# First block of a two-layer kernel: the recurrence, the index with its top-k and the attention run in pieces between the parts of one input product of 19 reordered groups

## Time and profile before

| What | Value |
|---|---|
| Median of 3 runs (lowest to highest) | 2316.65 us (2316.13 to 2317.55) |
| The profiled execution's own time | 2318.26 us |
| Its span | 2316.5 us |
| Mean granted clock of TensorE, share of full speed | 0.941 |
| PE busy / DVE busy / ACT busy / POOL busy | 92% / 62% / 38% / 1% |
| Input product, first to last matmul | 127.86 to 545.27 us |
| Output product g_o, first matmul | 718.04 us |

### The profile page before, as it was taken

The page is one execution under the profiler, slowest core; times in us unless marked ns, Lnnn a source line. Parts: engine busy times, 40 slices in busy tenths (PEclk is TensorE's granted clock), DMA queues, the critical chain, the costliest instruction groups (busy, mean ns, idle before and its releaser), DMA issues.

```text
span 2316.5 us, 23790 instructions
## 1 busy us (share of the span) xinstructions
PE 2122.0 (92%) x9261; PEld 1678.0 (72%) x9261; DVE 1438.8 (62%) x2254; ACT 884.3 (38%) x1070; POOL 21.5 (1%) x13
## 2 busy tenths in 40 slices
PE   6799999996697989999996779898999999999999
PEld 1278888885465867788783458777888888878887
DVE  4478655667837877787778676646544545444443
ACT  1134433444514344344440053435444444443332
POOL 0000000000200000000000000000000000000000
PEclk9889998998767999999997899998999999999999
DMA  9948755553003756576661015454556565655554
GB/s 349 379 164 296 277 190 168 199 192 122 1 1 94 220 156 206 186 223 202 202 198 48 0 37 189 151 188 133 193 186 194 184 196 185 196 167 200 189 193 163
DMA packets 208223, 406.34 MB, mean 175 GB/s; under 512 B 10809, under 2 KB 16369, under 8 KB 207729
## 3 DMA queue, kind: packets, MB, share of 16 engines
q1 hardware_dynamic: 203232, 397.24, 51.9%
q10 hardware_dynamic: 4882, 7.62, 1.0%
HBM read 402.74 MB, written 2.10 MB: 175 GB/s over the span
## 4 chain that ended last, share of the span: by engine, by line
PE 81%; DVE 10%; DMA 5%; ACT 2%; issue 1%; SPq 0%; DVEq 0%; ACTq 0%
PE ps L368 74%; PE pm L438 6%; DMA raw<-in_ada_w 3%; DVE raw_lo L346 2%; DMA raw<-in_w_in 1%; DVE mod_part L986 1%; DVE sc_i L1093 1%; PE pm L722 0%; PE pm L450 0%; ACT w_hi L337 0%; DVE sc_w L1105 0%; DMA decay<-in_decay 0%; DVE f_tmp L1221 0%; DVE xtmp L1336 0%; DVE lb_tmp L1113 0%
## 5 line engine op out<-in xcount | busy, mean ns | idle before, releaser
L346 DVE TENSOR_TENSOR raw_lo<-raw,w_hi 128x1024 fp32r<-128x1024 f32 x648 | 784.8, 1214 | 629.3 <-ACT w_hi L337 621.6
L337 ACT ACTIVATE w_hi<-raw 128x1024 fp32r<-128x1024 f32 x648 | 678.9, 1051 | 973.8 <-PE ps L368 927.6
L368 PE MATMUL ps<-w_hi,h_hi 128*128 128x512 f32 (+1 forms) x2336 | 920.1, 394 | 35.3 <-DVE h_lo L801 19.1
L368 PE MATMUL ps<-raw_lo,h_hi 128*128 128x512 f32 (+1 forms) x2336 | 915.3, 392 | 0.0
L368 PE MATMUL ps<-w_hi,h_lo 128*128 128x512 f32 (+1 forms) x2336 | 914.7, 392 | 0.0
L368 PEld LDWEIGHTS ps<-w_hi,h_hi 128*128 128x128 f32 x2336 | 445.5, 191 | 128.9 <-DVE h_lo L801 21.6
L368 PEld LDWEIGHTS ps<-w_hi,h_lo 128*128 128x128 f32 x2336 | 445.6, 191 | 92.2
L368 PEld LDWEIGHTS ps<-raw_lo,h_hi 128*128 128x128 f32 x2336 | 445.9, 191 | 90.3 <-issue 0.2
L368 PE MATMUL ps<-w_hi,hid_hi 128*128 128x512 f32 x256 | 99.9, 390 | 1.8 <-DVE raw_lo L346 1.8
L368 PE MATMUL ps<-w_hi,hid_lo 128*128 128x512 f32 x256 | 99.6, 389 | 0.0
L368 PE MATMUL ps<-raw_lo,hid_hi 128*128 128x512 f32 x256 | 99.6, 389 | 0.0
(11 more groups left out here) (291 smaller groups left out, 1225.6 us busy)
## 6 DMA issues: line engine op xcount, KB each, us to landing
raw<-in_w_in SPq DMA_DIRECT2D x140, 1024.0 KB, 5.2
raw<-in_w_ffn_gate SPq DMA_DIRECT2D x44, 1024.0 KB, 5.2
raw<-in_w_ffn_up SPq DMA_DIRECT2D x44, 1024.0 KB, 5.1
raw<-in_w_ffn_down SPq DMA_DIRECT2D x44, 1024.0 KB, 5.1
raw<-in_ada_w SPq DMA_DIRECT2D x32, 1024.0 KB, 7.5
raw<-in_w_out SPq DMA_DIRECT2D x32, 1024.0 KB, 5.1
proj<-in_ada_w SPq DMA_DIRECT2D x16, 1024.0 KB, 9.4
raw<-in_w_br_hyena SPq DMA_DIRECT2D x8, 1024.0 KB, 5.0
```

The source lines that it names most:

```text
L337: nc.scalar.activation(w_hi[:, p % HRING, :, 0:gm.width], raw[:, k % RING, e:e + HT, 0:gm.width], ACT.Copy).then_inc(hi_done, 1)
L346: nc.vector.tensor_tensor(raw_lo[:, k % RING, e:e + HT, 0:gm.width], raw[:, k % RING, e:e + HT, 0:gm.width], w_hi[:, p % HRING, :, 0:gm.wi ...
L368: mm = nc.tensor.matmul(ps[pair][:, t, 0:gm.width], l[:, tok], r[:, i, 0:gm.width], start=(k == 0 and q == 0), stop=(k == kt - 1 and q == 2))
```

## The change

The three Gemms become one, g_in, of 19 groups in the order r_f, r_q, r_i, (i_k, i_w), i_q, a_q, a_k, a_v, a_g, r_g. The work of the serial stage is cut into pieces, each with the number of the part beside which it is issued. PE does its piece after the 12 matmuls of the part; ACT and DVE do theirs LEAD = 3 parts later in their own order, which is the part on which they work while PE is about three behind. The list "chain" has no limit of time: whatever is due at a part is done at once.

```
+D_AT = (25, 29, 33, 40)
+TURN_AT = (36, 47)
+HEAD_AT = 50
+INDEX_AT = (86, 90, 104)
+QK_AT = 117
+K_SCALED_AT = 118
+AT_AT = 123
+MIX_AT = 145
+LEAD = 3
...
-    def step(self, part, share):
-        self.left = min(self.left + share, 2.0)
+    def step(self, part, share=1e9):
+        self.left = min(self.left + share, max(share, 2.0))
...
-        g_a = Gemm([(w1v, 0)], KT, 10)
-        g_s = Gemm([(w1v, I_K)], KT, 1, width=IDX_D + IDX_H)
-        g_r = Gemm([(w1v, R_Q)], KT, 8)
+        g_in = Gemm([(w1v, 0)], KT, len(GROUPS_IN), GROUPS_IN)
...
                 mm.then_inc(mm_done, 1)
+                if beside is not None:
+                    beside.step(p)
...
+            def block_one():
+                yield from recurrence()
+                yield from index()
+                yield from attend_beside()
+                for u in range(6):
+                    yield MIX_AT + u
+                    turn_mix(u)
```

PE's attention (a step each part, three units for one step spread over six parts; the order of the 16 steps is now by half of the heads):

```
+                for i in range(n + 6):
+                    yield AT_AT + i
+                    if i < n:
+                        t, h = AT_STEPS[i]
+                        mm(bank(pe, ("at1", "s", i), "v")[:, 0:at_keys(i)], qT1[:, h, t * P:t * P + P],
+                           kT1[:, h, 0:at_keys(i)]).then_inc(filled, 1)
+                    if 0 <= i - 3 < n:
+                        pe.wait_ge(sig("at1_weights"), i - 3 + 1)
...
+                    if 0 <= i - 6 < n:
...
```

DVE: the lower bound runs at the start (it was in the serial stage), its reciprocal as two halves; the lists and their shares; the head norm; the top-k (still eight rounds in one go, the yields in it cost nothing in the chain):

```
+            def lower_bound():
+                yield g_in.part(1)
+                dve.wait_ge(sig("lb_in"), 16)
+                v.tensor_tensor(lb_tmp, lb[:, 0], lb[:, 1], ALU.max).then_inc(sig("lb_max"), 1)
+                yield g_in.part(2, 1)
+                dve.wait_ge(sig("lb_sum"), 1)
+                for q in range(2):
...
+                yield HEAD_AT + 2 * NH + 1 + LEAD + 3
+                m = head_scale("or", qa, NH, HD)
...
-            beside = ((gate_work, 0.7), (head_work, 0.7))
-            groups(g_a, range(1, g_a.groups), None, beside)
...
+            beside = ((chain, 1e9), (gate_work, 0.7), (head_work, 1.2))
+            last = g_in.groups - 1
+            groups(g_in, range(1, last), None, beside)
```

ACT: groups are read from PSUM with their function (sigmoid, silu or copy) at once; the squares of q and k for the norm move from DVE (multiply and reduce) to ACT (32 instructions of 128 x 128 with a sum), the scaling of k too (16), that of q goes into the scores; DVE rotates q and k with tables that hold the gain:

```
+                f = ACT.Sigmoid if j < IN_RQ else ACT.Silu if j < IN_RI or j >= IN_AG else ACT.Copy
+                i = s.activation(proj[:, :, o:o + w], pair[:, :, 0:w], f)
...
+                for t in range(TT):
+                    yield D_AT[0] - 2 + LEAD + t
+                    act.wait_ge(sig("f_ready"), t + 1)
+                    s.activation(lf[:, t], kc[:, t], ACT.Ln).then_inc(sig("lf_ready"), 1)
```

SP: two slots instead of four for the chunks of the gate row, fetched one group later, each waiting for the chunk two before it; x is read a second time (2 MB) at the end of g_in, since the columns of q, k and of the recurrence now lie where x was. POOL no longer multiplies r_g by the gain:

```
-                for i in range(2 * j, min(2 * j + 2, ADA_GATE * RING)):
+                for i in range(2 * j - 2, 2 * j):
+                    if 0 <= i < ADA_GATE * RING:
...
+                if j == g_in.groups - 1:
+                    sp.wait_ge(filled, units[("at1", "s", len(AT_STEPS) - 1)][0] + 1)
+                    sp.dma_start(x_res[:], a["x"].rearrange("a (t p) n -> p (a t) n", p=P)).then_inc(sig("x_again"), 16)
```

More of the change, by code:

```diff
@@ L631, in _, with turn_mix_in @@
+            beside = Spare(block_one())
+            turn_h1 = turning([("h1", hbuf, KT)])
+            for j in range(g_in.groups):
+                multiply_group(pe, g_in, j, halves, turn_h1 if j == 0 else None, beside if j else None)
+            assert beside.over
+            def turn_mix_in(n):
+                if n in (2, 3):
+                    turn_mix(n + 4)
+                drained(("mix", n))
+            multiply(pe, g_o, halves, turn_mix_in)
             pe.wait_ge(sig("h2_rows"), 1)
@@ L1064, in queries_and_keys @@
+                dve.sem_inc(sig("ki_roped"), 1)
+                yield g_in.part(IN_IQ + 2, 3)
+                for j in range(2):
+                    evacuated(dve, g_in, IN_IQ + j)
                 for t in range(TT):
@@ L1172, in _ @@
[L1172 to L1181 removed]
+                dve.sem_inc(sig("qi_roped"), 1)
@@ new lines, in _ @@
+            mix = halves_in("mix", KT // 2)
+            for n in range(g_in.parts):
+                low(dve, g_in, last, n)
+                for work, share in beside:
+                    work.step(g_in.part(last, n), share)
+                if n >= MIX_AT + LEAD - g_in.part(last):
+                    next(mix)
+            assert chain.over and gate_work.over and head_work.over
+            for n in range(g_o.parts):
+                low(dve, g_o, 0, n)
+                if n == 1:
+                    gate_recurrence(1)
+                if n < 2:
+                    next(mix)
+                if n == 3:
+                    for _ in mix:
+                        pass
@@ new lines, in block_one @@
+            def block_one():
+                yield from recurrence()
+                yield from index()
+                yield from attend_beside()
+            chain, norm_work = Spare(block_one()), Spare(norms())
+            beside = ((chain, 1e9), (norm_work, 1.2))
+            last = g_in.groups - 1
+            for j in range(1, g_in.groups):
+                for n in range(g_in.parts):
+                    high(act, g_in, j, n)
+                    if n == HRING - 2:
+                        read_in(j - 1)
+                    for work, share in beside:
+                        work.step(g_in.part(j, n), share)
+                    if j == last and n >= MIX_AT + LEAD - g_in.part(last):
+                        highs(HT, HT * (n + g_in.part(last) - MIX_AT - LEAD))
@@ L1682, in _ @@
+            assert chain.over and norm_work.over
+            ahead = MIX_AT + LEAD - g_in.part(last)
+            for n in range(g_o.parts):
+                high(act, g_o, 0, n)
+                if n == 0:
+                    read_in(last)
+                if n < 2:
+                    highs(HT, HT * (g_in.parts - ahead + n))
+                if n == 3:
+                    for u in range(g_in.parts - ahead + 2, KT // HT):
+                        highs(HT, HT * u)
             groups(g_o, range(1, g_o.groups), None, squares_of("h2", lambda j: act.wait_ge(sig("h2_added"), j + 1)))
```

816 lines of the change are left out of this document (491 added, 325 removed).

## The result

| | before | after |
|---|---|---|
| Median (lowest to highest) | 2316.13 us (2295.54 to 2318.95, 13 runs) | 2290.09 us (2280.45 to 2295.23, 13 runs) |
| The profiled execution | 2318.26 us, span 2316.5 | 2285.51 us, span 2283.7 |
| Mean granted clock | 0.941 | 0.957 |
| PE / DVE / ACT / POOL busy | 92 / 62 / 38 / 1% | 92 / 63 / 40 / 1% |

The ratio is 0.9914, 95% interval 0.989 to 0.9938: faster by some 20 us. The forecast was 2261 us, 56 us faster; 2290 lies in the range of 2234 to 2294, so the sign and the range held and the size did not. Profile against profile the gain is 32.8 us, where 56 were forecast.

A forecast was written before the change was run, and what follows sets the result against it. PE bounds the input product; in the 172.8 us serial stage engines wait for each other. Terms: -177.4 (stage, g_o start) + 81.9 (pieces) + 7.4 (narrow-group clock) + 32 (stalls) = -56, giving 2261 us, range 2234 to 2294.

The forecast's parts named there:

- a gap of 8 us also lets the clock fall, +2: Parts 18 to 22, beside POOL's forget-gate work: 2 us added for a lower clock after the gap.
- the logarithm: Part 24: ACT's step with w_hi, table loads, a group copy and the first logarithm takes 5.7 us, stalling PE 2 us.
- the price of the pieces: PE's serial-stage work moved between product parts, priced at the upper clock: +81.9 us, bounds -5 and +10.
- The waits: PE stalls where much DVE or ACT work is due at once, parts 8 to 118 and g_o's seam: 32 us including +2 for clock.
- The narrow group: Parts 48 to 55, 80 columns: clock falls, and heads 0 to 2 beside it cost 2.5 us more each, +7.4.
- The first group of g_o: With six of eight units turned beforehand it loses its slow start: 22.7 us against 27.3, -4.6.
- Rival 1: DVE has its lead at part 17, only 12 us of single-step overhang remain: -76, 2241 us; chance 0.23.
- Rival 2: Two gate-row slots make ACT's first weight chunk late in groups 2 to 8: 21 us more, 2282 us; chance 0.11.
- Rival 3: Lower clock stays beside the heads, parts 56 to 67: 28 and 12 us more, 2301 us; chance 0.08.
- Rival 4: PSUM banks in attention and heads make PE wait at some 85 parts; at 1 us each 2346 us; chance 0.05.
- Rival 5: Nothing moves: a first wait at part 24 holds PE until the old chain is over; 2317 us; chance 0.01.
- would-show list: Signs expected: g_o starts near 667 us, raw_lo waits as listed, D, heads and attention at clock 1.00 except parts 50 to 56.

The follow-up runs named there:

- stall_doses: Kernel before with four bursts of 11, 13, 17 and 22 VectorE reciprocals put into product groups 2, 4, 6 and 8; 2368.68 us.
- gate_loads_spread: Changed kernel with each group's two gate-row loads issued behind weight chunks 1 and 3 of the group that uses them; 2286.87 us, ratio 0.9899.

## Why the forecast of the size was wrong

The parts of the sum, against the two profiles of the changed kernel. "Product" is the 417.4 us of the earlier trace rows less the 9.8 lost in it at the lower clock (2.9 at its start, 6.9 at the narrow group); "pieces" is what is left when waits and loss are taken off.

| | forecast | first profile | second |
|---|---|---|---|
| Start of the product | 127.9 | 129.9 | 127.6 |
| Product at full clock | 407.6 | 407.6 | 407.6 |
| Pieces at full clock | 81.9 | 91.4 | 90.2 |
| Waits | 30 | 35.6 | 36.6 |
| Lower clock at the start | 2.9 | 2.6 | 2.5 |
| Lower clock, narrow group and heads | 6.9 + 7.4 | 0 | 10.2 |
| Lower clock behind waits | 2 | 16.3 | 13.1 |
| First group of g_o | 22.7 | 26.5 | 26.5 |
| The rest | 1571.2 | 1573.8 | 1573.6 |
| Sum, the span | 2260.5 | 2283.7 | 2287.9 |

**The step that failed** is "a gap of 8 us also lets the clock fall, +2", counted once, for one stall of eight. In the first profile six waits have such a tail, in the second four, in all 16.3 and 13.1 us where the sum had 2: mis-sized by 11 to 14 us. The four doses show that a stall is enough for such a tail; they lost 2.1 to 3.0 us each, so the 6.3 behind the logarithm's wait are more than a stall alone accounts for, and what makes that one longer stays open. The prediction gave no row for the 2.

**The second** is the price of the pieces, 81.9 for 91.4. The upper bound I gave (+10, each of some 100 pieces draining PE for 0.1 us) was nearly the true value; the ten profiles of the changed kernel and its edits, with different waits and losses, give some 90 to 94 by the same subtraction. The price of the heads is not what was wrong: at clock 1.00 the eight took 28.3 us in stall_doses, where the forecast had 28.4. The excess stands at the seams. Here is a piece of the attention between two parts:

```profile
590.26 0.38 PE L475 MATMUL pm<-kT,qT 128*128 128x128 f32 x2
590.40 0.48 PE L394 MATMUL ps<-w_hi,h_hi 128*128 128x512 f32 x1
590.71 0.39 PE L394 MATMUL ps<-raw_lo,h_hi 128*128 128x512 f32 x1
590.94 0.40 PE L394 MATMUL ps<-w_hi,h_lo 128*128 128x512 f32 x1
```

The first wide matmul behind it starts 0.31 us before the second, where 0.227 is usual. It is 0.31 to 0.34 us in all 70 such places of the first profile that the records show at the upper clock, of 87 pieces in wide parts: 0.1 us each, some 8 to 9 us, and at about a quarter of the pieces another 0.1 stands ahead of them. That this is a drain of PE, as the forecast had it, is not shown; that it goes with each piece is.

**The waits** came near: 30 forecast, 35.6 and 36.6 measured, in part because an excess at the first places and a lack at the last balance. Place by place: parts 8 and 9, 2 for 3.0; the lower bound and POOL together 13 for 15.9; the logarithm 2 for 4.8; head norm 4 for 4.0; top-k 5 for 7.0; the rest 4 for 0.7. At the logarithm the list of ACT's step was complete, but the step began late, because its weights did:

```profile
221.03 2.01 ACT L363 ACTIVATE w_hi<-raw 128x1024 fp32r<-128x1024 f32 x2 [6.91 <-DMA raw<-in_w_in]
...
224.82 1.28 ACT L1826 ACT_TABLE_LOAD   x1
...
227.16 1.28 ACT L1840 ACT_TABLE_LOAD   x1
...
228.45 1.06 ACT L1840 ACTIVATE proj<-proj 128x1024 f32<-128x1024 f32 x1
...
230.36 1.04 ACT L1840 ACTIVATE proj<-proj 128x1024 f32<-128x1024 f32 x1
```

The price of a table load was rightly taken from the earlier trace rows: 1.28 us to the next instruction here too, and again loads on either side of the logarithm, against the 2.66 and the common set of the Trainium skill ("ScalarE: Activation LUTs", "What ACT_TABLE_LOAD costs" and "Table sets: the hidden batching unit").

**The narrow group.** +7.4 for three heads at the lower clock was in the sum. The first profile owes nothing of it, the second 10.2 with the group's own loss, against 14.3. The sum was thus 14 us too high here for the first profile. That is luck: without it the first profile would have missed the forecast by some 37 us instead of 23.

**The first group of g_o** was to lose its slow start wholly, and lost 0.8 of 4.6: three waits for raw_lo (1.31, 1.01, 0.93) stand in it, DVE doing the last two units' halves there. **The rest** is 2.6 and 2.4 us longer than the 1571.2 that the forecast leaves for it, and 3.0 when both kernels are counted from the same instruction of ACT: at the 3 I had allowed. Waits of PE make some 1.9 of it. It is also the size of the scatter: counted that way, four profiles of before have 1566.9 to 1570.8 us there, those of the changed kernel and its edits 1568.3 to 1573.8.

**The rivals.** Rival 1 (the cover holds) is out by the waits. Rival 2 exists in the trace (35.6 us of ACT's waits) and is worth some 3 us by gate_loads_spread, not 21. Rival 3 did not happen: behind the narrow group the clock is back within some 5 us. Rival 5 is out, all work moved. Rival 4 (banks): PE never waited on a reader in the attention; the one 0.7 us is for kT. Of the would-show list four lines failed: g_o began at 683 instead of 667, the heads in parts 50 to 56 stood at 1.00 in four of nine profiles, dec ran at 0.50 behind the logarithm's wait, and wide parts stood at 0.50 behind the waits, which the forecast had named as a sign of being wrong.

**The comparison.** All of this compares profiles, 32.8 us apart, where the ratio gives 20. The first profile lies 4.6 below the changed kernel's median; the rest is that some four in ten of before's executions run their heads' stretch faster, which three agreeing runs could not show.

## What to carry to other kernels

Look at the granted clock behind every stall of the tensor engine, and count what is lost there with the stall: here 2.1 to 3.0 us behind doses of 7 to 16 us, 0 to 3 behind waits of 1.7 to 4 us, nothing behind those of 0.6 to 1.6, and 3.4 to 6.5 where a wait of 2.5 to 4.8 us was followed by many matmuls of 2 columns. By these figures one long stall that is split into several of 3 us can cost more than it did whole (no run tried that), and steps without a limit per part make stalls of that length. Count 0.1 us for each small piece put between wide matmuls. Spread any step that is longer than the lead into the parts around it, and first ask if the step is needed in this form (a reciprocal of 6.6 us was two sigmoids of 1.05 us on an engine 40% busy). Where a kernel has a long stretch of small matmuls, take more than three runs before you trust the baseline.

## What was not expected of the hardware

- Small matmuls (128 columns or fewer, some of 32 to 64 rows) back to back ran a whole stretch of 47 us at clock 0.50 in some executions and in 28 us at 1.00 in another; with every matmul issued twice they took 94 us at 0.50 in the profiled execution, without the clock coming back inside, and by the times not in five of thirteen. The narrow group with heads beside it behaved alike.
- A DVE `tensor_scalar` that reads and writes SBUF is held by POOL as well. Four of them took 1.19 us in the kernel before and 5.43 beside two POOL instructions of 4.72 us together here:

```profile
155.36 4.72 POOL L2134 TENSOR_TENSOR proj<-proj,xtmp 128x1024 f32<-128x1024 f32 x2 [154.91 <-DVE xtmp L1140]
```
```profile
155.33 5.43 DVE L1292 TENSOR_SCALAR trig<-inv_f,pos_f 128x96 f32<-128x96 f32 x4
```

The forecast had only the page's word for this (the Trainium skill, "SBUF — State Buffer", on the shared port pair) and priced it at 2 us; the trace agrees with the page.
